# One product after another: the order of the matmuls in a dense output block, and when they wait for split weights

## The reference, cut to what matters

```
z = rms_norm(x) @ w_in                       # 1024 -> q, k, v, lru_x, lru_gate, merge gates
o = windowed attention over q, k, v          # 16 heads of 64, windows of 128
h = RG-LRU(conv(lru_x))                      # two 64x64 block gates per 64 channels, then a scan
x = x + (g_a * (o @ w_attn_out) + g_b * ((h * gelu(y)) @ w_lru_out)) @ w_o
gate, up = split(rms_norm(x) @ w_gate_up)    # 1024 -> 2 x 2816
x = x + (silu(gate) * up) @ w_down           # 2816 -> 1024
```

## Time and profile before

| | |
|---|---|
| median of three runs | 1777.89 us |
| span of the profiled execution | 1775.5 us |
| TensorE matmul busy | 1719.3 us, 97%, 10582 matmuls |
| TensorE weight load busy | 1656.5 us, 93%, 10582 loads |
| VectorE, GpSimd, ScalarE busy | 978.0, 659.6, 410.2 us |
| mean granted clock of TensorE | 0.990 |

### The profile page before, as it was taken

One profiled execution on the slowest core, in us unless ns is written; L12 is line 12 of the kernel. 1 busy time (PEld: TensorE's weight loads), 2 busy tenths in 40 slices (PEclk: granted clock), 3 DMA queues, 4 the chain that ended last, 5 costly groups with the idle time before them and its releaser, 6 DMA issues.

```text
span 1775.5 us, 30428 instructions
## 1 busy us (share of the span) xinstructions
PE 1719.3 (97%) x10582; PEld 1656.5 (93%) x10582; DVE 978.0 (55%) x1774; ACT 410.2 (23%) x1026; POOL 659.6 (37%) x600
## 2 busy tenths in 40 slices
PE   6999999899999999999979999999999999999999
PEld 5999999899998988888879999999999999999999
DVE  6686574549326885868786553342442443443435
ACT  4354244212215343343313221001001001010010
POOL 5755455232331222131374333332333332333331
PEclk9999999999999999999989999999999999999999
DMA  4111211121321202132333211111111111111112
GB/s 158 48 48 60 59 47 59 51 86 64 97 89 70 73 33 78 33 85 86 110 126 105 75 48 42 43 49 48 48 48 48 38 46 49 48 48 43 44 47 110
DMA packets 48912, 114.92 MB, mean 65 GB/s; under 512 B 14032, under 2 KB 25872, under 8 KB 48672
## 3 DMA queue, kind: packets, MB, share of 16 engines
q1 hardware_dynamic: 25168, 83.43, 14.9%
q10 hardware_dynamic: 23632, 29.93, 5.4%
HBM read 97.84 MB, written 15.76 MB: 64 GB/s over the span
## 4 chain that ended last, share of the span: by engine, by line
PE 84%; DVE 9%; issue 3%; ACT 2%; POOL 1%; DMA 0%; ACTq 0%; DVEq 0%; POOLq 0%; SPq 0%
PE bank L347 83%; DVE qstd L1248 2%; PE bank L537 1%; DVE acc L1138 1%; DVE mg L1390 1%; DVE qt L1262 1%; DVE x L1122 1%; DVE ti L1200 0%; ACT xc L765 0%; POOL wh L299 0%; DVE xc L1192 0%; DVE rt L1243 0%; POOL wl L301 0%; ACT aa L759 0%; DVE xc L1202 0%
## 5 line engine op out<-in xcount | busy, mean ns | idle before, releaser
L299 POOL TENSOR_SCALAR wh<-wraw 128x512 fp32r<-128x512 f32 x284 | 211.6, 745 | 1026.5 <-PE bank L347 1017.2
L347 PE MATMUL bank<-acth,wh 128*128 128x352 f32 x1728 | 571.0, 330 | 15.6 <-issue 5.7
L347 PE MATMUL bank<-acth,wl 128*128 128x352 f32 x1728 | 560.1, 324 | 0.0
L347 PE MATMUL bank<-actl,wh 128*128 128x352 f32 x1728 | 559.5, 324 | 0.0
L301 POOL TENSOR_TENSOR wl<-wraw,wh 128x512 fp32r<-128x512 f32 x284 | 402.5, 1417 | 41.1
L347 PEld LDWEIGHTS bank<-acth,wh 128*128 128x128 f32 x1728 | 327.3, 189 | 21.5 <-issue 16.6
L347 PE MATMUL bank<-n2h,wh 128*128 128x352 f32 x1056 | 341.2, 323 | 4.3 <-POOL wh L299 4.3
L347 PE MATMUL bank<-n2l,wh 128*128 128x352 f32 x1056 | 338.5, 321 | 0.0
L347 PE MATMUL bank<-n2h,wl 128*128 128x352 f32 x1056 | 338.3, 320 | 0.0
L347 PEld LDWEIGHTS bank<-actl,wh 128*128 128x128 f32 x1728 | 328.0, 190 | 3.3
L347 PEld LDWEIGHTS bank<-acth,wl 128*128 128x128 f32 x1728 | 327.4, 189 | 0.3
(11 more groups left out here) (148 smaller groups left out, 2049.9 us busy)
## 6 DMA issues: line engine op xcount, KB each, us to landing
wraw<-in_weights SPq DMA_DIRECT2D x142, 512.0 KB, 3.6
mb_scratch<-acc ACTq DMA_DIRECT2D x8, 528.0 KB, 2.7
ta_scratch<-tg ACTq DMA_DIRECT2D x24, 176.0 KB, 1.9
mg<-ta_scratch ACTq DMA_DIRECT2D x8, 528.0 KB, 4.6
mg<-mb_scratch ACTq DMA_DIRECT2D x8, 528.0 KB, 6.0
xr<-in_x ACTq DMA_DIRECT2D x24, 176.0 KB, 2.4
out_y<-acc SPq DMA_DIRECT2D x7, 528.0 KB, 2.7
acc<-in_x SPq DMA_DIRECT2D x2, 1408.0 KB, 13.0
```

The source lines that it names most:

```text
L299: nc.gpsimd.tensor_scalar(wh[:, u, c], wraw[:, u, c], 1.0, 0.0, ALU.mult, ALU.add).then_inc(split_done, 1)
L347: return nc.tensor.matmul(*args, **kw)
```

## The change

In `dense_block` the two inner loops change places: the product (`part` 0, 1, 2) is now outside and the chunk inside. A bank gets all eight chunks of high by high, then all eight of high weights by low input, then all eight of low weights by high input. The number of matmuls, their operands and the last one that raises the semaphore stay. The waits for weights are now one for each part of a half: high parts ahead of chunks 0 and 4 of part 0, low parts ahead of chunks 0 and 4 of part 2: four waits in a unit where there were two. `before` is called in part 0 alone.

```diff
-                for k in range(KC):
-                    if n == 0 and k % 4 == 0:
-                        weights(ahead, k // 4)
-                    if before:
-                        before(n, k)
-                    w = slice(k * P, (k + 1) * P)
-                    for lhs, rhs in ((wh, rh), (wh, rl), (wl, rh)):
-                        i = mm(out, lhs[:, slot, w], rhs[:, k, blk(n)], start=k == 0 and rhs is rh and lhs is wh,
-                               stop=k == KC - 1 and lhs is wl)
-                        if k == KC - 1 and lhs is wl:
+                for part, (lhs, rhs) in enumerate(((wh, rh), (wh, rl), (wl, rh))):
+                    for k in range(KC):
+                        if n == 0 and k % 4 == 0 and part != 1:
+                            wait(pe, split_done, 4 * plan.units.value(ahead) + 2 * (k // 4) + 1 + part // 2)
+                        if before and part == 0:
+                            before(n, k)
+                        w = slice(k * P, (k + 1) * P)
+                        i = mm(out, lhs[:, slot, w], rhs[:, k, blk(n)], start=k == 0 and part == 0,
+                               stop=k == KC - 1 and part == 2)
+                        if k == KC - 1 and part == 2:
                             i.then_inc(job.done[0], 1)
                         if each:
                             each()
```

## The result

The changed kernel took 1788.56 us (median of four), the kernel before 1777.31 us (median of four, 1774.42 to 1778.27). Three runs of the changed kernel took 1787.95 to 1789.13 us; the fourth took 3278.45 us at a mean granted clock of 0.914, against 0.991 in the others, and is left out of the ratio. The ratio is 1.006, with a 95% interval of 1.0043 to 1.0077: slower by 0.6%, some 11 us. The span of the profiled execution went from 1775.5 to 1786.1 us.

The account below looks back on a forecast made before the run. TensorE, busy 97% of the span, was taken to bound the kernel. From 1777.9 us: rate 0, waits +0.5, stalls -0.1, low input 0, predicted 1778.3 us; own range 1775 to 1781, 8-in-10 range 1769 to 1789.

Parts of the forecast that it names:

- the prediction's own sign: Prediction counts as wrong if the dense units' matmul rate moves by over half a nanosecond, in either direction.
- The rate: Dense units' 6624 matmuls: time per matmul unchanged, 0; bounds -9 us and +11 us.
- rival 1: Every dense block: different weights or stepping input addresses slow matmuls by up to 1.7 ns, giving 1781.6 to 1789; chance 0.22.
- a more broken order: Down projection, changing bank after 6 matmuls and taking two chunks in a row: costs only 0.5 ns each.
- The added waits: Dense units: 184 more waits for weights, mostly hidden by TensorE's queue running ahead; taken as +0.5 us.
- Rival 3: Attention stage: 20 added waits exposed, up to 3.4 us, giving 1781.7; chance 0.05.
- The finer waits: Two dense units stalled for GpSimd: separate high and low waits gain -0.1 us together, bounds -0.3 and +0.2.
- The two stalls: Dense units ready at 73.00 and 132.22: waits move behind the fourth matmul; gains nothing and 0.1 us.
- Rival 4: The stalls' whole 1.27 + 0.64 us go, giving 1776.4; shares the forecast's 0.50.
- The low input: First feed-forward block: eighth chunk's wait behind 7 matmuls instead of 21; nothing late, cost 0.
- Equal weights side by side: Dense units: giving up 2208 same-weight pairs costs nothing, since loads equalled matmuls (10582) before too.
- Rival 2: Dense blocks: equal inputs read chunk by chunk run at the shortest kind's pace, 1769 at -1.3 ns; chance 0.23.

Follow-up runs that it names:

- the waits alone: Kernel before in its old product order, with four waits in a unit, high and low parts apart: 1776.45 us, ratio 0.9999.
- new_order_old_waits: Changed kernel's order (eight chunks of one product in a row) with the two coarse waits of the kernel before: 1792.42 us, ratio 1.0082.

## Why the prediction was off, point by point

The measured time lies inside the wide range, 1769 to 1789, by less than half a microsecond, and outside the forecast's own, 1775 to 1781. That it lies inside is luck: the range took +1.6 ns on all 6624 matmuls for its end, while the rate grew by 2.8 ns and little over half of that sum reached the time. By the prediction's own sign, a rate that moves by over half a nanosecond, it was wrong.

- **The rate.** This step failed. I took 0, with a bound of +1.7 ns from the longest of the three kinds in the earlier trace rows. Measured: +2.8 ns in a unit and in an iteration. Of the cases, rival 1 came true, in its place (nearly every dense block) and in one of the two causes it named. Different weights at every matmul are nothing. The input stepping by a chunk each time is the right operand, but not the step costs: with 4352 bytes from chunk to chunk the same steps cost nothing. What costs is that the place changes. Chunks are 4224 bytes apart, 128 more than a multiple of 256, so the place flips between 32 and 160 with every chunk: after every third matmul before, after every matmul now. The means by kind could not bound that: an alternation of single matmuls appears in no row of before. What I took for a more broken order, the down projection, changes chunk only after three matmuls too, so its 0.5 ns could not show this cost. The addresses, which the code gives, would have told the two cases apart.
- **From rate to time.** 6624 matmuls at 2.8 ns would be 18.5 us; the span grew by 10.6. From 914 us on (50 of the 92 units, 10.1 us at 2.8 ns) the pieces grew by 2.55 + 1.63 + 1.60 + 1.61 + 1.46 = 8.9 us (the three middle ones are whole iterations). Before 914 us the kernel lost only 1.9 us: the luck of the clock hides 1.5, and the attention stage hardly pays. From its first step to the piece at 914 us the time grew by 0.35 us, from 386.17 to 386.52, with over 1000 touched matmuls in it. One reason is that VectorE holds the chain for long stretches there, as between 588.81 and 613.82 us before, where slower matmuls cost nothing:

```profile
588.81 3.59 DVE acc L1361
...
613.82 13.40 PE bank L347 x80
```

  The other shows between the steps. The start of an attention step and of the third one behind it, before, and then after:

```profile
533.99 0.59 PE L347 MATMUL bank<-kg,qt 128*128 128x256 f32 x2
...
542.79 0.59 PE L347 MATMUL bank<-kg,qt 128*128 128x256 f32 x2
```

```profile
535.57 0.59 PE L347 MATMUL bank<-kg,qt 128*128 128x256 f32 x2
...
544.40 0.59 PE L347 MATMUL bank<-kg,qt 128*128 128x256 f32 x2
```

  8.80 and 8.83 us for three steps with 33 dense matmuls between them, which at +2.8 ns would be 0.09 longer, not 0.03. It is similar behind a stall: the first block of the four feed-forward loop turns grew by 34 ns on average, 1.4 ns a matmul, and only the next ones by 2.8. So right behind an interruption the surcharge is smaller. Why, the runs don't show.
- **The added waits.** +0.5 was right in being next to nothing: the waits alone gave 0.9999. Rival 3, waits exposed in the attention stage, is out: the waits of weight loads for their own queue there are 11.0 us in 64 waits, as in the earlier trace rows.
- **The finer waits.** The two stalls went as worked out, the wait for the second high part in place of the first low one (0.3 and about 0 us gained, forecast 0.1). Rival 4 is out: the two waits are still 0.89 and 0.57 us, where they were 1.27 and 0.64. What I missed is that the same order with the old waits would have been 4 us slower, so that the waits are needed to keep the order from costing more.
- **The low input.** Right: no wait for L1398 in the first feed-forward block.
- **Equal weights side by side.** Right by the row: the 2208 repeats given up were worth nothing, and a kernel without any repeat took the time of before.
- **Rival 2** (a faster stream) is out for this layout, but for the five blocks at 158.3 to 158.5 ns. With a fixed place, blocks are faster than before only at place 32.

## What to carry to other kernels

When a loop order changes on a stream of back-to-back matmuls, write down the start address of the moving operand of each successive matmul, modulo 256, before and after. In this kernel a stride that is an odd multiple of 128 bytes was harmless while three matmuls in a row shared a chunk, and made each matmul 1.8% longer when the chunk changed at every one. Keeping the products of one chunk together avoids it. Padding the stride to a multiple of 256 avoids the alternation but fixes the place, and the place then decides: 32 and 160 gave the whole loss back, 0 and 128 gave nothing back (139.36 us an iteration). So choose the base together with the stride, and measure. And when an order wants data in another sequence than their maker delivers, check the granularity of the waits together with the order, not after it.

## What the runs showed of the hardware

- The rate of 128x128 by 352-column matmuls at full clock depends on where the input begins within 256 bytes, if that stays the same: 158.3 ns (3.80 us a block) at byte 32, 160.0 ns at 160 and 128, 162.1 ns at 0, with the absolute bytes by the layout's address. Four more places, read in the stages before the feed-forward at 160 ns within 0.2, are 64, 96, 192 and 224; their rows are not shown.
- If the place alternates between 32 and 160, the cost depends on how often: every third matmul 158.9 ns, a little under the mean of the two fixed places, 159.2; every second 159.9 (138.35 us an iteration, 0.55 over 137.80, on 576 matmuls); every one 161.7, in 215 of 220 blocks. The rest ran at 158.3 to 158.5 ns, and so did 14 of 215 such blocks in new_order_old_waits. What puts a stretch at the quicker rate is open.
- Right behind a stall or an attention step the alternation costs less, 1.4 and 0.9 ns a matmul.
- Repeating the stationary operand saves nothing (137.77 us an iteration with no repeats, 137.80 with them), and its address within a unit does not matter (139.39 against 139.40).
- Why the places differ is open. Only a column count of 352 and an alternation by 128 bytes were tried.
